# Four modulation blocks of the recurrent layer's second half, multiplied in the preparation of queries and keys instead of the readout

## What is computed

```
def adaln(cond, w, b):
    return jnp.split(jax.nn.silu(cond) @ w + b, 6, axis=-1)

for layer in range(DEPTH):                       # 0: attention + mLSTM, 1: RWKV
    sh_a, sc_a, gt_a, sh_m, sc_m, gt_m = adaln(c[:, None, :], ada_w[layer], ada_b[layer])
    ...
    x = x + gt_a * o_l                                             # o_l: the layer's mixer
    x = x + gt_m * squared_relu_mlp(modulate(x, sh_m, sc_m), ...)
```

## Time and profile before

| | us |
|---|---|
| median of 3 runs | 3368.64 (3364.41 to 3373.53) |
| profiled execution, its time | 3366.5 |
| profiled execution, its span | 3364.6 |
| mean granted clock of TensorE | 0.936 of 2.4 GHz |
| PE busy in the span | 2912.8 (87%) |
| DVE, ACT, POOL busy | 1352.2, 930.9, 315.6 |
| DMA moved | 681.01 MB, mean 202 GB/s |
| preparation (`abprep`), first step to last ACT copy | 206.9 to 248.9 |
| readout (`rwread`), first step to the bias add | 1546.5 to 1598.2 |

### The profile page before, as it was taken

How to read it: one execution, slowest core, us unless ns; L and a number is a source line. 1 busy time by engine, 2 the same in 40 slices (tenths; PEclk the granted TensorE clock), 3 DMA queues, 4 the chain that set the end, 5 groups by cost and what they waited for, 6 DMA issues and landing times. The chain is left out here.

```text
span 3364.6 us, 79115 instructions
## 1 busy us (share of the span) xinstructions
PE 2912.8 (87%) x34998; PEld 1945.4 (58%) x34998; DVE 1352.2 (40%) x2137; ACT 930.9 (28%) x1627; POOL 315.6 (9%) x253
## 2 busy tenths in 40 slices
PE   7988899999987788778899995785999899899995
PEld 4865568886665667664898875664333333333332
DVE  3355643334753654654556675454111001101112
ACT  3124432323323343331444453332010011001100
POOL 0021200000501231230000002202000000000001
PEclk8989899999997999997899998886999999999998
DMA  7272322223142100105454530065899999999996
GB/s 259 76 261 90 129 75 100 84 92 128 51 161 99 53 23 22 54 4 184 154 196 155 174 129 28 31 251 199 348 421 422 421 421 421 421 421 421 421 421 273
DMA packets 195158, 681.01 MB, mean 202 GB/s; under 512 B 25616, under 2 KB 40464, under 8 KB 145504
## 3 DMA queue, kind: packets, MB, share of 16 engines
q1 hardware_dynamic: 174992, 650.20, 49.5%
q10 hardware_dynamic: 18768, 22.95, 1.9%
q0 software_dynamic: 1152, 4.19, 0.4%
HBM read 651.86 MB, written 25.43 MB: 201 GB/s over the span
## 5 line engine op out<-in xcount | busy, mean ns | idle before, releaser
L3854 PE MATMUL experts_psum_gu<-ring,experts_x 128*32 128x512 f32 x3840 | 433.4, 598 | 37.6 <-DMA ring<-in_w_gu 37.6
L3972 DVE TENSOR_SCALAR experts_gate<-experts_psum_gu 128x768 f32<-128x768 f32 (+1 forms) x32 | 26.4, 825 | 857.8 <-PE experts_psum_gu L3854 857.8
L3854 PEld LDWEIGHTS experts_psum_gu<-ring,experts_x 128*32 128x32 f32 x3840 | 111.9, 110 | 340.8 <-issue 239.4
L3879 PE MATMUL experts_psum_down<-down_weights,experts_hiddenT 128*32 128x256 f32 x5120 | 286.5, 381 | 16.4 <-DMA down_weights<-in_w_down 13.1
L3879 PEld LDWEIGHTS experts_psum_down<-down_weights,experts_hiddenT 128*32 128x32 f32 x5120 | 159.1, 110 | 153.6 <-DMA down_weights<-in_w_down 35.5
L3916 ACT ACTIVATE experts_sigmoid<-experts_gate 128x768 f32<-128x768 f32 (+1 forms) x32 | 23.6, 739 | 589.4 <-DVE experts_gate L3972 589.4
L982 PE MATMUL mlp_psum_bank<-mlp_x_high,mlp_w_high 128*128 128x512 f32 (+1 forms) x512 | 175.3, 342 | 8.7 <-DVE xT_rounded L469 5.3
L982 PE MATMUL mlp_psum_bank<-xT_rounded,mlp_w_high 128*128 128x512 f32 (+1 forms) x512 | 175.0, 342 | 0.0
L315 DVE TENSOR_TENSOR ring_rounded<-ring,mlp_w_high 128x1024 fp32r<-128x1024 f32 x128 | 156.8, 1225 | 44.3 <-ACT mlp_w_high L310 44.3
L982 PE MATMUL mlp_psum_bank<-mlp_x_high,ring_rounded 128*128 128x512 f32 (+1 forms) x512 | 173.5, 339 | 0.0
L992 PE MATMUL mlp_psum_bank<-mlp_hidden_high,mlp_w_high 128*128 128x512 f32 (+1 forms) x512 | 172.3, 336 | 1.2 <-ACT mlp_relu L928 1.2
(11 more groups left out here) (766 smaller groups left out, 5913.6 us busy)
## 6 DMA issues: line engine op xcount, KB each, us to landing
ring<-in_w_gu SPq DMA_DIRECT2D x192, 1024.0 KB, 26.0
down_weights<-in_w_down SPq DMA_DIRECT2D x128, 1024.0 KB, 27.2
ring<-in_ada_w SPq DMA_DIRECT2D x72, 1024.0 KB, 10.1
ring<-in_mlp_w SPq DMA_DIRECT2D x64, 1024.0 KB, 7.0
xT<-in_w_gu SPq DMA_DIRECT2D x64, 1024.0 KB, 26.1
ring<-in_w_in SPq DMA_DIRECT2D x24, 1024.0 KB, 6.5
ring<-in_ab_w_in SPq DMA_DIRECT2D x12, 1024.0 KB, 10.2
ring<-in_w_rkv SPq DMA_DIRECT2D x12, 1024.0 KB, 6.9
```

What stands on the lines that cost most here:

```text
L3854: mm = nc.tensor.matmul(pg[32 * j:32 * j + 32, gr, :, :], x, strip(w, j), start=False, stop=(u == U - 1))
L3879: mm = nc.tensor.matmul(pd[32 * c:32 * c + 32, gr, :], hidT[:, a, gr, GROUP * v:GROUP * v + GROUP], w[:, a, C * c:C * c + C], start=(v == ...
L3972: v.tensor_scalar(G, pg[:, 0:groups, 0, :], SWI_LIMIT, None, ALU.min).then_inc(s_gt, 1)
```

## The change

The blocks 8 to 11 of layer 1 move from the readout's `Modulate` to the preparation's, behind its own eight. `ab_prepare` now takes a tuple of parts, as `rw_readout` did. The plan of the ring is moved with them, so that the order of loads stays the order of use. The preparation then runs 12 steps, the readout 4 (layer 2, blocks 0 to 3).

```diff
@@ ab_prepare
-        m = Modulate(g, ph, modulate)
+        m = Modulate(g, ph, *modulate)
@@ layer0
-            ab_prepare(g, pa, pb, small, rope, gates, bm, win, qT, kT, (0, 4, 8, a["adab_col"][0]))
+            ab_prepare(g, pa, pb, small, rope, gates, bm, win, qT, kT, ((0, 4, 8, a["adab_col"][0]), (1, 8, 4, a["adab_col"][1])))
@@ layer1
             rw_readout(g, fetch, y, coef, v, {"lw": lw[:, :], "lb": lb[:, :]}, sg0, sg1, g2a, g2b, ro,
-                       ((1, 8, 4, a["adab_col"][1]), (2, 0, 4, a["adab2_col"])))
+                       ((2, 0, 4, a["adab2_col"]),))
@@ program
         plan_ada(0, 4, 8)
+        plan_ada(1, 8, 4)
         plan_ada(1, 0, 8)
@@
             plan_cols(ring, a["w_rkv"][i], D, u)
-        plan_ada(1, 8, 4)
         plan_ada(2, 0, 4)
```

## The result

| | before | changed |
|---|---|---|
| median of 8 runs each, in one comparison | 3369.44 (3361.81 to 3373.53) | 3381.66 (3377.34 to 3393.14) |
| ratio, 95% interval | | 1.0043 (1.0027 to 1.0058) |
| profiled execution, its span | 3366.5, 3364.6 | 3378.46, 3376.5 |
| mean granted clock | 0.936 | 0.930 |
| preparation, start of the phase to the attention | 43.4 | 66.0 |

The change made the kernel 14.5 us (0.43%) slower, where +3.5 was forecast. Differences in us are the ratio times the median of before; here the two medians themselves lie 12.2 us apart.

What follows compares the result with a forecast made beforehand. It took full-queue loads to pace the preparation and PE's own list the readout. +21.7 - 18.2 = +3.5 us, so 3370.0 us for the profiled execution and 3372.1 for the median; range 3364 to 3381.

Steps and rivals of the forecast that it cites:

- Preparation, four blocks more (a loss): Preparation: four more blocks cost their loads in a full queue, 5.42 us each, +21.7 us in all (19.9 to 25.1).
- PE's work is hidden behind the loads at either clock: Preparation: a block costs PE 5.42 us at half clock or 3.0 at full, against 5.42 of load, so nothing extra.
- The tail ... I take 0: Preparation, work behind the last load: stays 8.0 us; bound of 0 to 2.6 us more, taken as 0.
- Readout, four blocks less (a gain): Readout: PE's list sets the end, so four blocks fewer end the phase 18.2 us earlier.
- Slower, by the clock: Rival: TensorE at half clock in both places, +27.7 in the preparation, readout gain only 14.1; net +13.6, 3382.2 us; chance 0.10.
- The product behind it starting as long after the readout as before: Sign behind the readout: the following product keeps its distance, its load covered by 4 us.
- Something outside of both phases, half to each side: 0.02: All other phases: chance 0.02 that something there decides, split evenly between slower and faster.
- The chance for slower: Whole kernel: chance 0.13 of ending slower by more than 0.3%, 10.1 us; same had 0.81, faster 0.06.

Runs made afterwards that it cites:

- the kernel with five memsets: The kernel before with five memsets of an unread tile at the end of the first phase, 6.0 us put in; 3382.46 us, ratio 1.0019.
- the blocks were there twice: The kernel before with the four blocks loaded and multiplied in the preparation and again in the readout; 3412.61 us, ratio 1.0107.
- loads alone: The kernel before with four more blocks loaded in the preparation, each freed by one two-column product; 3401.82 us, ratio 1.0079.
- the last order: The kernel before with readout step 2 ahead of the gate's first product pair, steps 3 to 5 behind one pair each; 3368.28 us, ratio 0.9978.

## Why the prediction was wrong

Both terms that the prediction priced came true. What failed is that it put every other phase at nothing and gave something outside a chance of 0.02: these phases move by more than the forecast's whole sum, and part of that comes with the change.

- **"Preparation, four blocks more (a loss)", 21.7 us: right in size.** +22.5 by the last copy; by means of profiles 65.6 (three with the change) against 43.3 (eight without), +22.3. The price of a load is confirmed by itself (5.41 to 5.43 us). "PE's work is hidden behind the loads at either clock" holds but for 1.8 us: the sum left out tile 0's turn, which with a block at half clock (5.42) makes 7.4 us of work against 5.42 of load. The Trainium skill's figure (DMA: Bandwidth & Descriptors, Specifications; 358 GB/s, an estimate of 23.4 us) was rightly set aside for the measured rate: 385 to 388 GB/s again.
- **"The tail ... I take 0": right by luck.** The folds took 1.95, as assumed. But the last step came 1.8 us late behind its load and the turns took 1.5 us less than before.
- **"Readout, four blocks less (a gain)", 18.2 us: right.** 17.7 in the first profile; by means 36.2 against 54.6 (five profiles with the readout of before), 18.4.
- **"Slower, by the clock", +13.6: not what happened**, though its time was nearly met. It wanted 25.1 + 2.6 us in the preparation and a readout gain of 14.1; neither came.
- **"The product behind it starting as long after the readout as before": right**, a little better. The turn behind the readout took 3.2 to 4.3 us instead of 4.6 to 4.9, in two of the three because it now starts at full clock.
- **"Something outside of both phases, half to each side: 0.02": this step failed.** The sum put all other phases at nothing, and its range left them no room. The untouched phases differ by up to 13.4 us in total between profiles of equal instructions. All phases from the attention on, readout left out, take 3061.5 us in the profile the prediction used, 3067.7 to 3074.9 in seven others of kernels that are alike there, and 3062.4 to 3073.5 in the three with the change. So the ledger of the first pair of profiles, which shows +7 outside, mostly shows a short profile of before.
- **A part of the excess does belong to the change.** The mLSTM rows take 20.2 to 21.0 us in all three profiles with the change, and 18.0 to 18.7 in all eight without, 2.3 us more on average. Changed kernel:

```profile
340.40 5.31 PE L737 MATMUL mlrows_psum_mod_row<-ring,silu 128*2 128x512 f32 x32 [2.45 <-DVE mlrows_psum_mod_row L712]
...
352.88 1.04 PE L737 MATMUL mlrows_psum_mod_row<-ring,silu 128*2 128x512 f32 x8 [2.40 <-DMA ring<-in_ada_w]
353.85 2.94 PE L723 MATMUL mlrows_psum_mod<-fold,mlrows_mod_row 128*128 128x2 f32 x16
```

  The same group and last half step in the kernel with five memsets, whose mLSTM rows are those of the kernel before:

```profile
325.28 3.62 PE L737 MATMUL mlrows_psum_mod_row<-ring,silu 128*2 128x512 f32 x32 [2.45 <-DVE mlrows_psum_mod_row L712]
...
335.22 1.04 PE L737 MATMUL mlrows_psum_mod_row<-ring,silu 128*2 128x512 f32 x8 [1.56 <-DMA ring<-in_ada_w]
336.19 2.71 PE L723 MATMUL mlrows_psum_mod<-fold,mlrows_mod_row 128*128 128x2 f32 x16
```

  The first group is at half clock (5.31 against 3.62) in two of the three; there the turn ahead of it ran at full clock, 6.9 in place of 8.6 us, and the two cancel. A last half step that waits 2.27 to 2.80 us instead of 1.17 to 1.75 is in all three. It is so too where products were doubled in the preparation (2.69) and where the blocks were there twice (2.81), but not with loads alone (1.58). What makes that load land later stands in the DMA record. In this phase one transfer of kind `instruction`, 16 KB on queue q8, passes in every profile. In the kernel with five memsets, DMA in 326 to 329 us (the phase begins at 324.3) and in 332 to 335 (columns: queue and kind, packets, MB, share of 16 engines):

```profile
q1 hardware_dynamic: 275, 0.24, 42.0%
q8 instruction: 1, 0.02, 1.9%
...
q1 hardware_dynamic: 592, 1.18, 104.4%
```

  In the changed kernel, in 341 to 344 (the phase begins at 339.4) and in 348 to 351:

```profile
q1 hardware_dynamic: 244, 0.18, 20.5%
...
q1 hardware_dynamic: 582, 1.16, 102.2%
q8 instruction: 1, 0.02, 2.3%
```

  In the nine profiles without products added to the preparation, this transfer comes 2.9 to 3.1 us into the phase, as or before its first load is issued, and the two halves of that load land 2.71 us apart (2.89 once). In the five with products added (three with the change, products doubled, blocks there twice) it comes at 8.3 to 10.4 us, takes 1.05 to 1.09 us, and passes while the DMA engines are full; there the halves land 3.8 to 4.2 us apart, and every later load is behind by as much. So about 1.2 of the 2.3 us are an instruction fetch that falls among the loads. That it is PE's, whose list has grown, is inferred from these five; in the kernel with loads alone, where PE has almost nothing more to run, it stays at 2.9. No kernel moved the fetch by itself. Attention is at its longer value in all three, and in three of eight without the change, on average 1.0 us; as shown above, that is the other side of shorter turns in the preparation.
- **The sum by means of profiles, all phases counted:** +22.3 (preparation) - 18.4 (readout) - 1.9 (everything from the attention on, readout left out: 3068.1 for three, 3070.1 for eight) = +2 us. The last term is uncertain by 4 us. Within it mLSTM rows have +2.3, attention +1.0, the turns behind readout and attention -1.0 and -0.9, and merge and turn -3.1 (44.7 against 47.8), which is a phase with two values as well. The forecast's +3.5 agrees with this sum.
- **The sum by times is higher.** Measured were +14.5, +5.7 and +7.8; weighted by their intervals that is +9, with 3 us to either side (an estimate). The two sums differ mostly because profiles are single executions: the three profiled ones of the changed kernel lie 4.5 us on average under the medians of their runs, the eight others 1.5 us over theirs. Put right by these 6 us, the profiles give +8. So the change costs some 8 to 9 us, 4 to 5 more than the two places account for (+3.9). Of these mLSTM rows hold 2.3; where the others lie is open. The rest of the first comparison, some 5 us over +9, is twice its uncertainty (5.4 us of spread and 8 runs a side give 2.7) and stays unsettled. The comparisons were not made on one chip.
- **The range** reached to 3381, its upper end being +9.5 and 3 us of spread, and the median came out at 3381.66. The level of the base isn't to blame: in this comparison the kernel before had 3369.4, 0.8 over the 3368.6 used. But that level isn't fixed either. In the other three comparisons the same kernel has medians of 3379.5, 3376.3 and 3375.7; these 77 executions together have 3376.5 (3367.0 to 3391.1) and a standard deviation of 5.3. A median of three is so uncertain by some 4 us, a comparison of eight runs with eight by 5, and the unknown size of all other phases comes on top. The chance for slower should have been well above 0.13.

## What to carry to other kernels

Price moved weight blocks by the queue's measured rate where the queue is full, and by PE's own list where it isn't; both held here within 1 us. Price the clock of what stands between the blocks too, here a turn of 1.95 us instead of 1.07. Look for places where the queue is idle rather than count how many blocks stand where: the same blocks between the gate's products gained 7 to 15 us, in three comparisons of two orders, where moving four of them away lost. When the terms nearly cancel, compare two or three profiles of the same program first, phase by phase: what phases of equal instructions differ by is the floor under any forecast.

## What the hardware showed that was not expected

- **Equal instructions, two lengths.** The attention takes 58.3 us (five profiles) or 59.7 to 60.0 (three) up to the same point of the same program; state space to delta rule 139.4 to 149.6; the recurrence 528.2 to 533.6. In the attention the cause is visible: the clock falls to half behind a wait of 3.44 us, or doesn't. The Trainium skill (TensorE: Matmul & The Clock Gate, What's actually happening) says of the slow start of a kernel's matmuls that it is run-variable. The trace shows the same in the midst of a kernel, with 2.02 and 3.51 us for the same 16 records. The same section of the Trainium skill puts the penalty of the ramp under 1% of a typical kernel's span. Here all half clock together costs more: by the trace's record of the granted clock PE is busy for 281 us at half clock in the first profile of before and for 304 in the second; if such work takes twice its time (an estimate), that is 141 and 152 us, 4% of the span. Their difference, 11 us, is near that of the two spans (9.3), and more than the change is worth.
- **An instruction fetch can hold up a load.** 16 KB of instructions that pass among 1024 KB loads make the halves of one land 3.8 to 4.2 us apart instead of 2.7, where the same transfer costs nothing 6 us earlier, with the queue only starting. This fits all fourteen profiles; no kernel tested it alone.
- **Time follows the mean granted clock.** Over the 77 executions of the kernel before, time and clock have a correlation of -0.72, 2.2 us for each 0.001 of the clock. A kernel that is 0.2% faster can't be told from a run with a luckier clock by a few executions.
- **Half clock while busy.** In the readout PE waits 1.94 us for `v_lat`, then runs the gate's f32 products and the next step without a gap and still has 0.50 from 1555 to 1575, then full clock, in the kernel before. With steps between it rises near 1576, or already near 1573 in the second profile. In the last order, where no wait stands ahead of the gate, its first pair runs at full clock (1.12 us instead of 2.07 for two records), and the clock falls behind the two waits for loads. The forecast took the half clock of this place over from the earlier trace rows, which held. The reason of the half clock here is open.
